# Inverting the unit triangular matrices of an RWKV-7 layer: a chain of block factors with crossed array halves in place of doubling levels

## What is computed

```
def _rwkv7_step(state, inp):
    r_t, w_t, k_t, v_t, a_t, b_t = inp
    sa = jnp.einsum('bhvk,bhk->bhv', state, a_t)
    state = (state * w_t[:, :, None, :] + sa[..., None] * b_t[:, :, None, :]
             + v_t[..., None] * k_t[:, :, None, :])
    return state, jnp.einsum('bhvk,bhk->bhv', state, r_t)
```

## Time and profile before

| | |
|---|---|
| median of 3 runs | 1294.11 us (1293.96 to 1295.61) |
| profiled execution, its own time | 1292.58 us |
| its span (first to last instruction) | 1290.8 us |
| mean granted TensorE clock | 0.972 of full speed |
| PE, DVE, ACT, POOL busy | 92%, 57%, 19%, 7% of the span |
| chain that ended last, by engine | PE 82%, DMA 8%, DVE 5%, ACT 2% |

### The profile page before, as it was taken

One profiled execution on the slowest core, in us unless ns is written; L12 is line 12 of the kernel. 1 busy time (PEld: TensorE's weight loads), 2 busy tenths in 40 slices (PEclk: granted clock), 3 DMA queues, 4 the chain that ended last, 5 costly groups with the idle time before them and its releaser, 6 DMA issues.

```text
span 1290.8 us, 20413 instructions
## 1 busy us (share of the span) xinstructions
PE 1181.2 (92%) x8767; PEld 861.0 (67%) x8767; DVE 734.8 (57%) x1181; ACT 247.5 (19%) x427; POOL 92.5 (7%) x86
## 2 busy tenths in 40 slices
PE   6999999899876669999999999899999889999997
PEld 5855644556433334996588888667779884788886
DVE  5547521223211113665788777776966667877774
ACT  5412201221000003433100000435222011100000
POOL 2010000010000000120000000000300532000000
PEclk9999999999988889999999999999989999999999
DMA  9653135187999999532855560336100318656500
GB/s 343 217 190 130 66 119 207 66 319 301 421 421 417 422 421 398 188 140 98 293 176 185 193 196 1 98 131 212 41 3 4 101 36 268 234 184 195 195 1 32
DMA packets 106497, 247.24 MB, mean 192 GB/s; under 512 B 7121, under 2 KB 61408, under 8 KB 93986
## 3 DMA queue, kind: packets, MB, share of 16 engines
q1 hardware_dynamic: 106212, 245.71, 52.2%
q0 software_dynamic: 144, 0.15, 0.0%
q10 hardware_dynamic: 46, 0.01, 0.0%
HBM read 244.80 MB, written 1.05 MB: 190 GB/s over the span
## 4 chain that ended last, share of the span: by engine, by line
PE 82%; DMA 8%; DVE 5%; SPq 2%; ACT 2%; issue 1%; POOL 0%; DVEq 0%
PE bank L483 14%; PE bank L485 14%; PE bank L484 14%; PE bank L348 9%; DMA arena<-expert_w_gate 8%; PE bank L334 6%; PE bank L2442 4%; PE bank L1351 4%; PE bank L1366 2%; SPq L304 1%; PE bank L2336 1%; PE bank L1402 1%; PE bank L2418 1%; PE bank L1793 1%; PE bank L446 1%
## 5 line engine op out<-in xcount | busy, mean ns | idle before, releaser
L483 PE MATMUL bank<-work_rounded,work_rounded 128*128 128x512 f32 (+2 forms) x704 | 275.7, 392 | 9.7 <-DVE work_rounded L1727 5.2
L485 PE MATMUL bank<-work_rounded,work_rounded 128*128 128x512 f32 (+2 forms) x704 | 271.0, 385 | 0.0
L484 PE MATMUL bank<-ring_w_rounded,work_rounded 128*128 128x512 f32 (+2 forms) x576 | 222.1, 386 | 0.0
L483 PEld LDWEIGHTS bank<-work_rounded,work_rounded 128*128 128x128 f32 x704 | 132.2, 188 | 35.8 <-issue 5.7
L485 PEld LDWEIGHTS bank<-work_rounded,work_rounded 128*128 128x128 f32 x704 | 132.2, 188 | 24.4
L484 PEld LDWEIGHTS bank<-ring_w_rounded,work_rounded 128*128 128x128 f32 x576 | 109.1, 189 | 18.7 <-issue 0.2
L348 PE MATMUL bank<-arena 128*128 128x512 f32 x256 | 112.1, 594 | 3.1 <-ACT arena L1152 1.4
L1351 PE MATMUL bank<-arena 128*32 128x256 f32 x896 | 71.8, 441 | 44.9 <-DMA arena<-expert_w_gate 36.6
L1727 DVE TENSOR_TENSOR ring_w_rounded<-arena,work_rounded 128x1024 fp32r<-128x1024 f32 x84 | 102.9, 1225 | 2.9
L1245 ACT ACTIVATE arena<-bank 128x256 f32<-128x256 f32 x52 | 20.0, 385 | 416.3 <-PE bank L485 336.4
L1726 DVE CAST work_rounded<-arena 128x1024 fp32r<-128x1024 f32 (+1 forms) x140 | 93.7, 669 | 0.3
(11 more groups left out here) (416 smaller groups left out, 1630.2 us busy)
## 6 DMA issues: line engine op xcount, KB each, us to landing
arena<-expert_w_up SPq DMA_DIRECT2D x29, 1024.0 KB, 21.5
arena<-expert_w_down SPq DMA_DIRECT2D x28, 1024.0 KB, 26.2
arena<-expert_w_gate SPq DMA_DIRECT2D x27, 1024.0 KB, 17.3
arena<-ffn_w_gate SPq DMA_DIRECT2D x22, 1024.0 KB, 5.5
arena<-ffn_w_up SPq DMA_DIRECT2D x22, 1024.0 KB, 8.1
arena<-ffn_w_down SPq DMA_DIRECT2D x22, 1024.0 KB, 5.0
arena<-hy_w_in SPq DMA_DIRECT2D x12, 856.0 KB, 12.5
arena<-w_in SPq DMA_DIRECT2D x8, 1024.0 KB, 13.7
```

The costliest lines, as they stand in the source:

```text
L483: nc.tensor.matmul(out, lhsT[0], rhs[0], start=first, stop=False)
L484: nc.tensor.matmul(out, lhsT[0], rhs[1], start=False, stop=False)
L485: return nc.tensor.matmul(out, lhsT[1], rhs[0], start=False, stop=last)
```

## The change

The inverse is written as a product of factors, one per block size. Level by level a turned product RT and the inverse Yi are multiplied by the level's masked block factor E, in one matmul with RT and Yi side by side as 128 moving columns.

- Constants: the masks `rwlev` and `rwlevT` become unit matrix minus level mask, and the first block of `rwmask` is negated. `products_dve` adds the unit matrix into NM in place and makes Yi from it by one mask: two DVE operations as before.
- Xi and PM give way to RT (the same place as Xi) and two buffers EL for the factors (the second one lies in the front of UG's place). ACT copies X2 to EL[0].
- Levels 0 to 5 (LEVELS = 6). Level 0: Q0 and RY0 by `blocks_pe`. Levels 1 to 4: Q and RY by the new `crossed_pe`, into a pair of banks each (Q in ring D, RY in ring A), where the chunk half r of the operands and the head parity x pick the four quarters of the array. The moving operand has 64 columns for Q, 128 for RY of levels 1 to 3 and 64 for RY4. Level 5: RY5 by `blocks_pe`.
- DVE takes only Q out: one 128x512 per group in level 0, two 128x256 in levels 1 to 4, each times a mask, into the other EL buffer. ACT takes RY out (new `level_act`): one 128x512 copy per group in levels 0 and 5, two 128x512 copies into RT and Yi in levels 1 to 3, two 128x256 copies into Yi in level 4, the pairs only when the second bank is full.
- SP's hold on the `w_ro` pieces waits for Q0, Q1 and Q2 of tile 1 instead of dY0, dY1 and dY2.

```diff
-        LEVELS = 5
+        LEVELS = 6
...
+        def crossed_pe(pe, ring, name, half, lhs, rhs, out):
+
+            pair = [fill(pe, ring, f"{name}.{half}.{r}") for r in range(2)]
+            for j in range(4):
+                for r, rows in enumerate(HALVES):
+                    for x, cols_ in enumerate(HALVES):
+                        h = 8 * half + 2 * j + x
+                        mm = nc.tensor.matmul(out(pair[r], cols_, j), lhs(rows, h), rhs(rows, h), start=True, stop=True)
+                        if j == 3 and x:
+                            mm.then_inc(full[ring], 1)
+
         def level_pe(pe, t, lv):
+
+            E = EL[lv % 2]
+            one_block = lambda ps, c, j: ps[c, j * HD:(j + 1) * HD]
             for half in range(2):
-                await_moved(pe, f"dX{lv - 1}.{t}.{half}" if lv else f"X2.{t}.{half}")
-                blocks_pe(pe, "D", f"P{lv}", t, half, lambda w, h: NM[t][w, h, 0:CH], lambda w, h: Xi[w, h])
-            for half in range(2):
-                await_moved(pe, f"P{lv}.{t}.{half}")
-                if lv:
-                    await_moved(pe, f"dY{lv - 1}.{t}.{half}")
-                if lv < LEVELS - 1:
-                    blocks_pe(pe, "D", f"dX{lv}", t, half, lambda w, h: Yi[t][w, h], lambda w, h: PM[w, h])
-                blocks_pe(pe, "D", f"dY{lv}", t, half, lambda w, h: PM[w, h], lambda w, h: Yi[t][w, h])
+                if lv == 0:
+                    await_moved(pe, f"X2.{t}.{half}")
+                    blocks_pe(pe, "D", "Q0", t, half, lambda w, h: NM[t][w, h, 0:CH], lambda w, h: E[w, h])
+                    blocks_pe(pe, "A", "RY0", t, half, lambda w, h: E[w, h], lambda w, h: NM[t][w, h, 0:CH])
+                    continue
+                crossed_before = lv > 1
+                await_moved(pe, f"Q{lv - 1}.{t}.{half}.1" if crossed_before else f"Q0.{t}.{half}")
+                await_moved(pe, f"RY{lv - 1}.{t}.{half}.1" if crossed_before else f"RY0.{t}.{half}")
+                if lv == LEVELS - 1:
+                    blocks_pe(pe, "A", f"RY{lv}", t, half, lambda w, h: E[w, h], lambda w, h: Yi[t][w, h])
+                    continue
+                crossed_pe(pe, "D", f"Q{lv}.{t}", half, lambda r, h: RT[r, h], lambda r, h: E[r, h], one_block)
+                if lv < LEVELS - 2:
+                    crossed_pe(pe, "A", f"RY{lv}.{t}", half, lambda r, h: E[r, h],
+                               lambda r, h: two_blocks(r, RT_AT + h * HD, YI_AT[t] + h * HD),
+                               lambda ps, c, j: ps[c, :].rearrange("p (b j n) -> p b j n", b=2, j=4)[:, :, j])
+                else:
+                    crossed_pe(pe, "A", f"RY{lv}.{t}", half, lambda r, h: E[r, h], lambda r, h: Yi[t][r, h], one_block)
...
+        def level_act(act, t, lv):
+            for half in range(2):
+                if lv in (0, LEVELS - 1):
+                    ps = take(act, "A", f"RY{lv}.{t}.{half}")
+                    to = Yi[t] if lv else RT
+                    nc.scalar.copy(flat(to[:, 8 * half:8 * half + 8]), ps[:, :]).then_inc(moved["A"], 1)
+                    continue
+                peek(act, f"RY{lv}.{t}.{half}.1")
+                for r in range(2):
+                    ps = take(act, "A", f"RY{lv}.{t}.{half}.{r}")
+                    if lv < LEVELS - 2:
+                        nc.scalar.copy(turned_blocks(half, r, YI_AT[t]),
+                                       ps[:, :].rearrange("p (b j n) -> p b j n", b=2, j=4)).then_inc(moved["A"], 1)
+                    else:
+                        nc.scalar.copy(Yi[t][:, 8 * half + r:8 * half + 8:2],
+                                       ps[:, 0:256].rearrange("p (j n) -> p j n", j=4)).then_inc(moved["A"], 1)
...
         def level_dve(dve, t, lv):
             V = nc.vector
+            E, mask = EL[(lv + 1) % 2], C("rwlev")[:, lv * CH:(lv + 1) * CH]
             for half in range(2):
-                ps = take(dve, "D", f"P{lv}.{t}.{half}")
-                V.tensor_tensor(PM[:, 8 * half:8 * half + 8], eight(ps), bc(C("rwlev")[:, lv * CH:(lv + 1) * CH], 8, 1),
-                                ALU.mult).then_inc(moved["D"], 1)
...
+                if lv == 0:
+                    ps = take(dve, "D", f"Q0.{t}.{half}")
+                    V.tensor_tensor(E[:, 8 * half:8 * half + 8], eight(ps), bc(mask, 8, 1), ALU.mult).then_inc(moved["D"], 1)
+                    continue
+                for r in range(2):
+                    ps = take(dve, "D", f"Q{lv}.{t}.{half}.{r}")
+                    V.tensor_tensor(E[:, 8 * half + r:8 * half + 8:2], ps[:, 0:256].rearrange("p (j n) -> p j n", j=4),
+                                    bc(mask, 4, 1), ALU.mult).then_inc(moved["D"], 1)
```

More of the change, by code:

```diff
@@ L85, in _constants @@
     incl_c = ii[:, None] <= np.arange(CH)[None, :]
[L86 removed]
+    parts["rwmask"] = np.concatenate([-1.0 * strict_c, incl_c, strict_c, incl_c], 1).astype(float)
     mid = blk * CH + CH // 2 - 1
@@ L102, in _constants @@
         b *= 2
-    parts["rwlev"] = np.concatenate([np.concatenate(lv[1:], 1)] * 2, 0).astype(float)
-    parts["rwlevT"] = np.concatenate([lv[0].T] * 2, 0).astype(float)
+    eye = np.eye(CH)
+    parts["rwlev"] = np.concatenate([np.concatenate([eye - m for m in lv[1:]], 1)] * 2, 0)
+    parts["rwlevT"] = np.concatenate([eye - lv[0].T] * 2, 0)
     parts["strictP"] = (i[:, None] < i[None, :]).astype(float)
@@ L293, in stream @@
                     if step:
-                        peek(sp, f"dY{step - 1}.1.1")
+                        peek(sp, ("Q0.1.1", "Q1.1.1.1", "Q2.1.1.1")[step - 1])
                 if (slots[0] >= SLOTS and name != "late_const") or name.startswith("f1"):
@@ L2217, in build @@
         MV = [R0[:, 2048:3072].rearrange("p (h n) -> p h n", h=RH), view(2048, RH, HD)]
-        Xi = RB[:, 0:1024].rearrange("p (h n) -> p h n", h=RH)
+        RT = RB[:, 0:1024].rearrange("p (h n) -> p h n", h=RH)
         Yi = [RB[:, 1024 * (1 + t):1024 * (2 + t)].rearrange("p (h n) -> p h n", h=RH) for t in range(T)]
-        PM = RB[:, 3072:4096].rearrange("p (h n) -> p h n", h=RH)
+        EL = [RB[:, o:o + 1024].rearrange("p (h n) -> p h n", h=RH) for o in (3072, 4096)]
         UG = RB[:, 4096:6144].rearrange("p (h n) -> p h n", h=RH)
@@ L2228, in build @@
         NM_AT = (in_ring(4096), in_work(4096))
+        RT_AT = in_ring(4 * SLOT)
+        YI_AT = tuple(in_ring(4 * SLOT + 1024 * (1 + t)) for t in range(T))
         def two_blocks(w, first, second):
@@ L2234, in build, with turned_blocks @@
         HALVES = (slice(0, CH), slice(CH, P))
-        LEVELS = 5
+        LEVELS = 6
+        def turned_blocks(half, row, second):
+            one = arena[:, RT_AT + (8 * half + row) * HD:RT_AT + (8 * half + row + 1) * HD]
+            return bass.AP(tensor=one.tensor, offset=one.offset,
+                           ap=[one.ap[0], [second - RT_AT, 2], [2 * HD, 4], [1, HD]])
         NP_ = RH // 2
@@ L2469, in chunks_pe @@
             for half in range(2):
-                await_moved(pe, f"dY{LEVELS - 1}.{t}.{half}", f"Mv.{t}.{half}")
+                await_moved(pe, f"RY{LEVELS - 1}.{t}.{half}", f"Mv.{t}.{half}")
                 for g in (2 * half, 2 * half + 1):
@@ L2601, in rwkv_act @@
             inverse_start_act(act, 0)
+            for lv in range(LEVELS):
+                level_act(act, 0, lv)
             turn_act(act, 1)
@@ L2604, in rwkv_act @@
             inverse_start_act(act, 1)
+            for lv in range(LEVELS):
+                level_act(act, 1, lv)
             chunks_act(act, 1)
@@ L2617, in inverse_start_act @@
             for half in range(2):
-                for name, to in (("Mv", MV[t]), ("X2", Xi)):
+                for name, to in (("Mv", MV[t]), ("X2", EL[0])):
                     ps = take(act, "A", f"{name}.{t}.{half}")
                     nc.scalar.copy(flat(to[:, 8 * half:8 * half + 8]), ps[:, :]).then_inc(moved["A"], 1)
+        def level_act(act, t, lv):
[14 more added lines that the diff above has]
+                                       ps[:, 0:256].rearrange("p (j n) -> p j n", j=4)).then_inc(moved["A"], 1)
         def chunks_act(act, t):
@@ L2752, in rwkv_dve @@
             products_dve(dve, 0)
-            for lv in range(LEVELS):
+            for lv in range(LEVELS - 1):
                 level_dve(dve, 0, lv)
@@ L2803, in products_dve @@
                 h8 = slice(8 * half, 8 * half + 8)
-                links["dve"](V.tensor_tensor(Yi[t][:, h8], NM[t][:, h8, 0:CH], bc(C("rwlevT"), 8, 1), ALU.mult))
-                V.tensor_tensor(Yi[t][:, h8], Yi[t][:, h8], bc(C("eye2"), 8, 1), ALU.add).then_inc(sem("Y2"), 1)
+                links["dve"](V.tensor_tensor(NM[t][:, h8, 0:CH], NM[t][:, h8, 0:CH], bc(C("eye2"), 8, 1), ALU.add))
+                V.tensor_tensor(Yi[t][:, h8], NM[t][:, h8, 0:CH], bc(C("rwlevT"), 8, 1), ALU.mult).then_inc(sem("Y2"), 1)
         def level_dve(dve, t, lv):
             V = nc.vector
+            E, mask = EL[(lv + 1) % 2], C("rwlev")[:, lv * CH:(lv + 1) * CH]
             for half in range(2):
```

(5 more changed lines are left out.)

## The result

The changed kernel takes 1277.87 us (median of 4 runs, 1276.53 to 1282.01) against 1294.86 (4 runs): ratio 0.9873, interval 0.9847 to 0.9898, which is 16.4 us less (17.0 between the medians). Timed twice more, beside the experiments, the same kernel stood at 0.9877 (0.9855 to 0.9900) and 0.9904 (0.9884 to 0.9924). It is faster, as forecast, but by two thirds of the 25.5 us; 1277.87 lies 0.9 us above the range.

A forecast was written before the change was run, and what follows sets the result against it. PE was taken to bound both tiles' levels: tile 0 -9.7 and tile 1 -15.8 give -25.5 us, from 1292.58 to 1267.1, plus 1.5 for the median of the runs: 1268.6 us, range 1265 to 1277.

The forecast's parts named there:

- the 25.5 us: Whole kernel: the forecast saving, 9.7 us from tile 0's levels and 15.8 from tile 1's.
- the range: Whole kernel: forecast time between 1265 and 1277 us.
- Rival D: Both tiles' levels: shorter bursts with waits drop PE's clock to 1.2 GHz, slower than before at 1300.6 us; chance 0.03.
- Rival B: RY evictions: ACT becomes the bound, copies into 64-element pieces costing 1.00 instead of 0.50, total 1276.4 us; chance 0.12.
- my 1.08: Levels 1 to 3: duration of ACT's pair of 512-column RY copies, 1.08 us.
- The moments and the variance: Tile 1's levels: this DVE work stays hidden, paid for by the additions DVE lost.
- POOL is done in time: Tile 0's norm on POOL: done at 1039.2, with 6 to 7 us of slack, costing nothing.
- The 0.85 that I had in front of level 2: Tile 1, after the scan: PE waits 0.85 us for DVE before level 2, the change's largest wait.
- the price of a crossed bank: Q1 to Q4 and RY4: 32 crossed 64-column records cost 0.50 us, at Z's 15.5 ns each.
- the 25 ns rule: Crossed 64-column banks: start-to-start never below about 25 ns, so 0.80 us a bank and some 5 us less good.
- Rival C: Q1 to Q4 and RY4: an issue limit makes crossing buy nothing for 64 columns, total 1276.8 us; chance 0.08.
- cost nothing: SP's `w_ro` loads in tile 1: last piece out at about 1021.8, landing 5.2 later, long before 1046, no cost.

The follow-up runs named there:

- the first experiment: The changed kernel with RY1 to RY3 split into two crossed matmuls of 64 moving columns each, 192 more records per tile: tile 0's levels 25.02 us.
- the uncrossed kernel: The changed kernel with the merged RT and Yi operand and as many records, but without crossing: tile 0's levels 25.5 us.
- the paired kernel: The changed kernel with Q1 to Q4 made for two neighbouring heads at once, half the records for Q: 1284.93 us, ratio 0.9924.
- the half RY: The changed kernel with the update of Yi left out of RY1 to RY3, as many records: tile 0's levels 21.07 us.
- the first late loads: The changed kernel with the four `w_ro` loads held back until after tile 1's levels: 1282.76 us, ratio 0.9918.

## Why the prediction was right and wrong

**Right.** PE bounded both stretches; both got shorter, and nothing behind them took the gain back. Rival D did not come: of the windows above only one is near the lower level, at 0.78 for 6 us (0.72 for the run of 209 records in it), and the others are at 0.94 or more. Rival B did not come: in the change ACT's pair into 64-element pieces takes 1.07 for my 1.08.

```profile
967.34 1.07 ACT L2669 COPY arena<-bank 128x512 f32<-128x512 f32 x2 [1.53 <-PE bank L2470]
```

The moments and the variance hide in DVE's idle time (a wait of 0.28), the scan costs PE 0.48 where I had 0.5, and POOL is done in time (tile 0's norm at 1038.60, its transposes at 1045.82). The 0.85 that I had in front of level 2 can't be told from the gap of 1.10.

**The step that failed is the price of a crossed bank, "its 64 records take 1000.56 - 999.57 = 0.99 us, 15.5 ns each, so 32 cost 0.50"**, carried over from one burst to a whole stage. The burst is true; but a burst of 64 can live on instructions that are already there, and the levels use 704 in a row (the first gap comes behind nearly 300). What bounds a long run is one block of 128 records per 3.6 to 4.0 us (the means of eight profiles), 28 to 31 ns per record. With 29.7 tile 0 comes to 704 x 0.0297 = 20.9 (measured 20.80), and the saving of 192 records to 5.7 (measured 5.8). That both fit so well is partly luck: the same rate gives 26.6 for the 896 records of the first experiment, which took 25.02, since a stage starts with blocks at hand and ends inside one. The kernel before ran at 26.60 / 896 = 29.7 ns, which hid this floor: it was bound by the array (uncrossed records take 29 ns in the uncrossed kernel too, 0.93 us for 32, where the packets come only every 5.3 us), and its supply was just fast enough, with packets 3.7 us apart and no gap. The prediction's estimate by the 25 ns rule, some 5 us less good, would have come out nearer, but by chance: the bursts do run at 15.5 ns. Rival C ("an issue limit") named the right family and got 0.08; I priced it per crossed instruction, where it is a rate over all of them. Its signs were in the trace I read. PE stood still, called issue, for 0.62 us inside the second burst of Z, and for 0.64 us in tile 1's levels beside a load:

```profile
1005.46 0.32 PE L2512 MATMUL bank<-arena 64*64 64x64 f32 x2 [0.62 <-issue]
...
1033.93 2.43 PE L2442 MATMUL bank<-arena 64*64 64x64 f32 x76 [0.64 <-issue]
```

Of the 4.05 us missing in tile 0, the gaps are 0.83 + 0.74 + 0.75 + 1.17 = 3.49. The rest, 0.56, is about what RY's size makes for six banks: 1.03 in the paired kernel, where I took 0.93 out of 0.93 to 1.10.

**Tile 1** misses 28.19 - 20.15 = 8.04: gaps of 6.33, RY's size again about 0.6; the 1.1 left over I put down to the stretch at clock 0.78, which no run here separates. Here a second step failed, that the `w_ro` loads "cost nothing": I asked only whether they land in time, not what they delay. With the loads elsewhere, tile 1's levels are 3.7 to 4.2 us shorter (24.0, 23.7 and 24.0 for 28.2, 27.6 and 27.7). In the kernel before the same loads cost 0.9 us, so most of this loss came with the denser levels of the change. Where the loads went they cost something too, and in no pair of kernels that differ by the loads alone are the totals clearly told apart.

The range's upper end, 1277, came from B and C one at a time, and neither came as priced; that the time stands only 0.9 us above it is chance. Both stretches as measured give 1268.6 + 4.0 + 8.0 = 1280.6; the median of 1277.87 is 2.7 less, which no stretch explains and which lies inside the 5.5 us between the change's own runs.

## What to carry to other kernels

Beside array time, evictions and ways back, count the instructions of each dense stretch: here 256 per 3.8 us, a float32 matmul being four of them (two records and two weight loads). Where a stretch already runs at that rate, fewer columns, crossing or faster evictions buy nothing. Fewer and wider matmuls take the gaps away, but only pay while the array time stays under the supply: with all of Q paired tile 0's levels took 22.43 us for 20.80, with half of it 19.61 for 20.27, one profile each and less than their spread. A price taken from a short burst holds for a burst. Bulk loads beside such a stretch are not free even if they are early (3.7 to 4.2 us here), and moving them helps only if they find a place where PE is not dense.

## What the runs showed of the hardware

PE's instructions come in packets of 16 KB (1.15 MB in 70), and while PE waits for them its gaps end 3.4 to 4.1 us apart. In the profiles read packet by packet (three of the change; the split RY, the half RY and the first late loads) each gap ends 2.3 to 2.8 us after a packet, and the next packet moves 1.0 to 1.7 us behind the gap. Beside 1 MB loads (DMA share 0.82 in the window above) it moved up to 2.7 to 3.5 us behind it, and the change's gaps grow from 0.7 to 1.2 us to as much as 2.2 to 2.8. The Trainium skill, "Runtime: NRT & Kernel Launch" (Instruction fetch mechanics), has the blocks at 16 KiB or 256 instructions, with which the traces agree, and calls the cost of crossing into the next "mostly hidden", with which they do not: 3.5 of 20.8 us in tile 0. What fills the 2.3 to 2.8 us between packet and gap's end was not tried.

A stationary operand of 64 rows and 128 columns with 128 moving columns takes 68 ns a record (1.09 / 16) with the two row halves alternating, a 64x64 one over four quarters with 128 columns 32 ns (1.03 / 32). The stretch at the lower clock is not bound to the change. The kernel before has one in tile 1's levels in both its profiles (192 records in 7.36 us at 0.77). Of the change's three profiles two have it there (209 records in 6.20 us at 0.72 and 5.96 at 0.71), behind waits of up to 2.30 and 2.75; the third has waits of 2.20 and 1.51 there and stays at 1.00, but its first 32 records of the product with `w_ro` take 15.71 us at 0.89 in place of 14.02 at 1.00. What decides it is open.
